# A ring of 13 one-megabyte parts for the expert weights, 96 places for the second busiest expert, and down weights read as two adjacent rows per partition

## The reference, cut to what matters

```
logits = t @ router                      # 256 x 1024 @ 1024 x 8
top_logits, top_idx = top_k(logits, 2)
gates = softmax(top_logits)
combine = sum(one_hot(top_idx, 8) * gates[..., None], axis=1)
for e in range(8):                       # D_EXPERT = 3584
    out += combine[:, e:e+1] * ((silu(t @ w_gate[e]) * (t @ w_up[e])) @ w_down[e])
```

## Time and profile before

| | us |
|---|---|
| median of 3 runs | 3119.64 (3118.27 to 3120.79) |
| the profiled execution's own time | 3116.49 |
| its span | 3114.6 |
| TensorE busy in the span | 2967.0 (95%) |
| VectorE, ScalarE busy | 1220.9 and 482.5 |
| moved by DMA | 637.05 MB, mean 205 GB/s |
| HBM read | 632.70 MB |

### The profile page before, as it was taken

One profiled execution on the slowest core, in us unless ns is written; L12 is line 12 of the kernel. 1 busy time (PEld: TensorE's weight loads), 2 busy tenths in 40 slices (PEclk: granted clock), 3 DMA queues, 4 the chain that ended last, 5 costly groups with the idle time before them and its releaser, 6 DMA issues.

```text
span 3114.6 us, 48006 instructions
## 1 busy us (share of the span) xinstructions
PE 2967.0 (95%) x20333; PEld 2077.3 (67%) x20333; DVE 1220.9 (39%) x2557; ACT 482.5 (15%) x1080; POOL 109.9 (4%) x122
## 2 busy tenths in 40 slices
PE   7999998999999999999999999998999999989987
PEld 3566666588697677696786795876667667445443
DVE  2566766457476433466465375232000100100101
ACT  2332333010010123200221200221000000000001
POOL 1111112000000000000000000000000000000000
PEclk8999999999999999999999999998999999999999
DMA  7333116465455522355310365324999899999996
GB/s 255 117 109 129 55 55 254 166 215 163 135 185 168 161 69 74 94 195 171 104 52 21 107 205 176 115 61 177 367 386 381 327 387 382 371 393 389 360 394 256
DMA packets 361238, 637.05 MB, mean 205 GB/s; under 512 B 11950, under 2 KB 190741, under 8 KB 353725
## 3 DMA queue, kind: packets, MB, share of 16 engines
q1 hardware_dynamic: 355677, 612.49, 55.6%
q0 software_dynamic: 5344, 21.46, 2.1%
HBM read 632.70 MB, written 1.20 MB: 204 GB/s over the span
## 4 chain that ended last, share of the span: by engine, by line
PE 78%; DMA 11%; DVE 4%; SPq 2%; ACT 2%; issue 2%; DVEq 1%; PEld 1%; PEldq 0%; ACTq 0%
PE PS L1087 11%; PE PS L1646 7%; PE PS L1107 7%; PE PS L4140 7%; DMA scratch<-in_moe_wu 5%; PE PS L1040 4%; DMA W<-in_moe_wu 4%; PE PS L4201 3%; PE PS L4187 2%; PE PS L4147 2%; SPq L3998 2%; PE PS L710 2%; PE PS L2222 2%; PE PS L3594 2%; PE PS L1121 2%
## 5 line engine op out<-in xcount | busy, mean ns | idle before, releaser
L1646 PE MATMUL PS<-XT,WH 128*128 128x512 f32 x512 | 241.4, 597 | 1.7 <-ACT XT L487 1.7
L4140 PEld LDWEIGHTS PS<-scratch,W 128*128 128x128 f32 x1792 | 207.5, 194 | 32.1 <-issue 32.1
L4140 PE MATMUL PS<-scratch,W 128*128 128x128 f32 x1792 | 210.1, 277 | 8.2 <-DMA W<-in_moe_wu 8.2
L4160 PE MATMUL PS<-W,scratch 128*32 128x256 f32 x2688 | 151.1, 383 | 12.9 <-DMA W<-in_moe_wu 12.9
L4160 PEld LDWEIGHTS PS<-W,scratch 128*32 128x32 f32 x2688 | 96.9, 111 | 70.5 <-issue 26.9
L1015 DVE TENSOR_TENSOR scratch<-scratch,PS 128x128 f32<-128x128 f32 x56 | 16.1, 288 | 322.2 <-ACT scratch L1005 322.2
L1087 PE MATMUL PS<-XT,W 128*128 128x128 f32 x1024 | 128.2, 280 | 12.8 <-DVEq L1260 12.8
L1040 PE MATMUL PS<-XT,W 128*128 128x256 f32 x640 | 139.6, 379 | 0.0
L1087 PE MATMUL PS<-scratch,W 128*128 128x128 f32 x1024 | 135.5, 275 | 0.0
L1646 PEld LDWEIGHTS PS<-XT,WH 128*128 128x128 f32 x512 | 89.2, 192 | 69.1 <-issue 66.6
L1040 PEld LDWEIGHTS PS<-XT,W 128*128 128x128 f32 x640 | 121.4, 190 | 18.9 <-issue 2.9
(11 more groups left out here) (620 smaller groups left out, 4805.8 us busy)
## 6 DMA issues: line engine op xcount, KB each, us to landing
W<-in_moe_wg SPq DMA_DIRECT2D x56, 1024.0 KB, 8.5
W<-in_moe_wu SPq DMA_DIRECT2D x56, 1024.0 KB, 12.9
W<-in_moe_wd SPq DMA_DIRECT2D x56, 1024.0 KB, 9.8
XT<-in_moe_wg SPq DMA_DIRECT2D x56, 1024.0 KB, 11.4
scratch<-in_moe_wu SPq DMA_DIRECT2D x56, 1024.0 KB, 14.4
OT<-in_moe_wd SPq DMA_DIRECT2D x56, 1024.0 KB, 14.0
W<-in_ada_w SPq DMA_DIRECT2D x36, 1024.0 KB, 7.0
W<-in_ffn_w_gate SPq DMA_DIRECT2D x66, 512.0 KB, 4.9
```

What stands on the lines that cost most here:

```text
L1646: mm = k.nc.tensor.matmul(k.PS[:, n % 2, :], k.gdn_w[n][:, kb, :], k.XT[:, kb, :], start=kb == 0, stop=kb == KB - 1)
L4140: mm = nc.tensor.matmul(k.PS[:, 4 + f, w * SLOTS:(w + 1) * SLOTS], slots[w].wide[:, kb, c:c + P], k.xte[:, MANY, kb, :], start=kb == 0, st ...
L4160: mm = k.nc.tensor.matmul(k.PS[j * GROUP:(j + 1) * GROUP, 4 + g // 2, g % 2 * L:g % 2 * L + L], k.xte[:, MANY, kb, g * GROUP:(g + 1) * GRO ...
```

## The change

It replaces the expert stage's loads, buffers and order of work.

- The room of the four slots becomes a ring of 13 parts of 1 MB (2048 floats in each of 128 partitions): 7 in `W`, 2 each in `XT` and `OT` and 2 in `scratch`. Each load waits only until the part that it overwrites is used (`k.used`, one count per part, in the order in which TensorE works), and TensorE waits for each part by itself (`landed`).
- A pair has 4 turns instead of 7: three of 1024 hidden columns and one of 512 (`WIDTHS`). A part of up weights holds gate and up of one block of 128 input rows, 1024 columns each (rows of 4 KB), or of two blocks, 512 columns each.
- A part of down weights in a turn of 1024 holds, in each partition, two adjacent rows of the matrix, 8 KB that lie together in HBM. It is issued as two loads of 64 partitions each. In a turn of 512 it is two loads of 128 partitions with rows of 4 KB, as before.
- All ups of both kinds come first in a turn, then all downs. Gathers, the scatters of the pair before and the turned gates stand at fixed places between MANY's up parts of the first two turns.
- All tokens are stationary in groups of 32: four groups in pair 0 (128 places), three in pairs 1 to 3 (96), two for FEWER (64). `FULL_PAIRS` is 1. PSUM banks are given anew; the down sums are added to `ye` on VectorE once per turn.
- The branch for what has no place gets a ninth round, for rank 1.

```diff
-FULL_PAIRS = 2
+FULL_PAIRS = 1
-PAIR_ROUNDS = EXPERT_PAIRS * E_TURNS
+WIDTHS = (1024, 1024, 1024, 512)
+PART = 2048
+RING = 13
+UP_FILLS = [KB * w // 1024 for w in WIDTHS]
+DOWN_FILLS = [w // 256 for w in WIDTHS]
+STEP_FILLS = [2 * (u + d) for u, d in zip(UP_FILLS, DOWN_FILLS)]
+PAIR_FILLS = sum(STEP_FILLS)
...
+def expert_ups_sync(k, sp, pair, turn, kind, e):
+    ups, _ = expert_weights(k)
+    width, first = WIDTHS[turn], sum(WIDTHS[:turn])
+    kbs = 1024 // width
+    for i in range(UP_FILLS[turn]):
+        fill = fill_at(pair, turn, "up", kind, i)
+        if fill >= RING:
+            sp.wait_ge(k.used, fill - RING + 1)
+        to = k.ring[fill % RING].rearrange("p (kb w n) -> p kb w n", kb=kbs, w=2)
+        for w in range(2):
+            src = ups[w][:, ds(e, 1), kbs * i:kbs * i + kbs, first:first + width].rearrange("p e kb n -> p (e kb) n")
+            sp.dma_start(to[:, :, w, :], src).then_inc(k.ring_in[fill % RING][0], 16)
+
+def expert_downs_sync(k, sp, pair, turn, kind, e):
+    _, downs = expert_weights(k)
+    whole = k.t["moe_wd_1_2"].rearrange("e (b p f) n -> p e b (f n)", p=P, f=2)
+    block = sum(WIDTHS[:turn]) // P
+    for i in range(DOWN_FILLS[turn]):
+        fill = fill_at(pair, turn, "down", kind, i)
+        if fill >= RING:
+            sp.wait_ge(k.used, fill - RING + 1)
+        if WIDTHS[turn] == 1024:
+            for half in range(2):
+                src = whole[:, ds(e, 1), block // 2 + i, :].rearrange("p e n -> p (e n)")
+                sp.dma_start(k.ring[fill % RING][ROWS[half], :], src[ROWS[half], :]).then_inc(k.ring_in[fill % RING][0], 16)
+            continue
+        to = k.ring[fill % RING].rearrange("p (b n) -> p b n", b=2)
+        for f in range(2):
+            b = block + 2 * i + f
+            sp.dma_start(to[:, f:f + 1, :], downs[:, ds(e, 1), b:b + 1, :].rearrange("p e b n -> p (e b) n")
+                         ).then_inc(k.ring_in[fill % RING][0], 16)
...
+def expert_up_tensor(k, pe, pair, turn, kind, i):
+    fill = fill_at(pair, turn, "up", kind, i)
+    width = WIDTHS[turn]
+    kbs, part = 1024 // width, width // 4
+    pe.wait_ge(*landed(k, fill))
+    weights = k.ring[fill % RING].rearrange("p (kb w n) -> p kb w n", kb=kbs, w=2)
+    for n in range(kbs):
+        kb = kbs * i + n
+        for g in range(groups_of(kind, pair)):
+            for j in range(4):
+                mm = k.nc.tensor.matmul(k.PS[j * GROUP:(j + 1) * GROUP, 4 * kind + g, 0:2 * part],
+                                        k.xte[:, kind, kb, g * GROUP:(g + 1) * GROUP],
+                                        weights[:, n, :, j * part:(j + 1) * part], start=kb == 0, stop=kb == KB - 1)
+    mm.then_inc(k.used, 1)
...
 def duo_step_tensor(k, pe, pair, turn):
+    for i in range(UP_FILLS[turn]):
+        expert_up_tensor(k, pe, pair, turn, MANY, i)
...
+    if n:
+        pe.wait_ge(*k.turn_dve.at("y1", n - 1))
+    for i in range(UP_FILLS[turn]):
+        expert_up_tensor(k, pe, pair, turn, FEWER, i)
+        if i == 2:
+            expert_flip_tensor(k, pe, pair, turn, MANY)
+    pe.wait_ge(*k.turn_act.at("ht0", n))
+    if n:
+        pe.wait_ge(*k.turn_dve.at("y0", n - 1))
+    for i in range(DOWN_FILLS[turn]):
+        expert_down_tensor(k, pe, pair, turn, MANY, i)
+        if i == (0 if last else 1):
+            expert_flip_tensor(k, pe, pair, turn, FEWER)
+            if last and pair + 1 < EXPERT_PAIRS:
+                duo_gather_tensor(k, pe, pair + 1, MANY)
+    pe.wait_ge(*k.turn_act.at("ht1", n))
+    for i in range(DOWN_FILLS[turn]):
+        expert_down_tensor(k, pe, pair, turn, FEWER, i)
+        if last and i == 0 and pair + 1 < EXPERT_PAIRS:
+            duo_gather_tensor(k, pe, pair + 1, FEWER)
```

More of the change, by code:

```diff
@@ L3969, with groups_of, fill_at, landed @@
 MANY, FEWER = range(2)
-def turn_slots(k, kind, n):
-    base = MOE_BASE if kind == MANY else (0, 0)
-    return k.expert_slots[2 * kind:2 * kind + 2], [n + b for b in base]
+def groups_of(kind, pair):
+    return 2 if kind else 4 if pair < FULL_PAIRS else 3
+def fill_at(pair, turn, what, kind, i):
+    at = pair * PAIR_FILLS + sum(STEP_FILLS[:turn]) + i
+    if what == "down":
+        return at + 2 * UP_FILLS[turn] + kind * DOWN_FILLS[turn]
+    return at + kind * UP_FILLS[turn]
+def landed(k, fill):
+    sem, base = k.ring_in[fill % RING]
+    return sem, base + 32 * (fill // RING + 1)
+def used(k, pair, turn, what, kind):
+    fills = UP_FILLS if what == "up" else DOWN_FILLS
+    return k.used, fill_at(pair, turn, what, kind, fills[turn] - 1) + 1
 def expert_weights(k):
@@ L3989, in moe_sync @@
                    for rank in (pair, pair + MANY_RANKS)]
-        for turn in range(E_TURNS):
+        for turn in range(len(WIDTHS)):
             for kind, e in enumerate(experts):
[L3992 to L4002, removed]
+                expert_ups_sync(k, sp, pair, turn, kind, e)
+            for kind, e in enumerate(experts):
+                expert_downs_sync(k, sp, pair, turn, kind, e)
@@ L4005, in more_sync @@
 def more_sync(k, sp):
[L4006 to L4009, removed]
+    sp.wait_ge(k.used, EXPERT_PAIRS * PAIR_FILLS)
     with sp.Fori(0, EXPERTS) as e:
         with sp.Fori(0, E_TURNS) as j:
[L4012 to L4016, removed]
@@ L4121, in scatter_tensor @@
     else:
-        pe.wait_ge(*k.ga_act.at("tr", min(e + 1, EXPERTS - 1)))
+        pe.wait_ge(*k.ga_act.at("tr", min(e + 1, NE - 1)))
         pe.wait_ge(*k.sc_dve.at("y", e))
     scatter_products(k, e % 2, tile).then_inc(*k.sc_pe.done(f"sc{tile}"))
[L4127 to L4149, removed]
@@ L4152, in tri_up_tensor @@
[L4152 to L4164, removed]
@@ L4167, in tri_flip_tensor @@
[L4167 to L4191, removed]
@@ L4194, in few_up_tensor @@
[L4194 to L4202, removed]
-                                        slots[w].wide[:, kb, s * ROUND:(s + 1) * ROUND],
-                                        start=kb == 0, stop=kb == KB - 1)
-        mm.then_inc(*slots[w].pe.both("up0", "up1"))
@@ new lines, with expert_down_tensor @@
+DOWN_PLACES = {
+    4: [(half, g, f, g, half) for f in range(2) for half in range(2) for g in range(4)],
+    3: [(0, j, f, g, half) for f in range(2) for j, (g, half) in enumerate(((0, 0), (1, 0), (2, 0), (0, 1)))]
+    + [(1, j, f, g, 1) for j, (f, g) in enumerate(((0, 1), (0, 2), (1, 1), (1, 2)))],
+    2: [(0, 2 * half + g, f, g, half) for f in range(2) for half in range(2) for g in range(2)],
+}
+def expert_down_tensor(k, pe, pair, turn, kind, i):
+    fill = fill_at(pair, turn, "down", kind, i)
+    groups, blocks = groups_of(kind, pair), WIDTHS[turn] // 512
+    last = DOWN_FILLS[turn] - 1
+    pe.wait_ge(*landed(k, fill))
+    weights = k.ring[fill % RING].rearrange("p (b n) -> p b n", b=2)
+    places = DOWN_PLACES[groups]
+    for n, (bank, j, f, g, half) in enumerate(places):
+        at = ((2 * i + f) % blocks * groups + g) * P + (2 * i + f) // blocks * GROUP
+        opens = (bank, j) not in [q[0:2] for q in places[:n]]
+        closes = (bank, j) not in [q[0:2] for q in places[n + 1:]]
+        mm = k.nc.tensor.matmul(k.PS[j * GROUP:(j + 1) * GROUP, 5 if kind else 6 + bank, :], k.ht[kind][:, at:at + GROUP],
+                                weights[:, f, half * 512:(half + 1) * 512], start=i == 0 and opens, stop=i == last and closes)
+    mm.then_inc(k.used, 1)
@@ L4577, in duo_step_vector @@
+def duo_step_vector(k, dve, pair, turn):
+    first = turn == 0 and pair
+    if first:
+        duo_scatter_vector(k, dve, pair - 1, MANY, 0)
+        duo_scatter_vector(k, dve, pair - 1, MANY, 1)
+        duo_scatter_vector(k, dve, pair - 1, FEWER, 0)
     if turn == 2 and pair + 1 < EXPERT_PAIRS:
@@ L4579, in duo_step_vector @@
             duo_choice_vector(k, dve, pair + 1, kind)
-    if turn == E_TURNS - 1:
-        for kind in range(2):
-            duo_sum_vector(k, dve, pair, kind)
+    expert_hidden_vector(k, dve, pair, turn, MANY)
+    if first:
+        duo_scatter_vector(k, dve, pair - 1, FEWER, 1)
+    expert_hidden_vector(k, dve, pair, turn, FEWER)
+    for kind in range(2):
+        expert_sum_vector(k, dve, pair, turn, kind)
 def moe_vector(k, dve):
```

336 lines of the change are left out of this document (119 added, 217 removed).

## The result

The changed kernel takes 3297.65 us, the kernel before beside it 3120.22 us (3118.27 to 3122.96): a ratio of 1.0562, interval 1.0541 to 1.0582, so 5.6% slower. It was forecast slower, by 70 us and not by 177, and the time lies above the range.

A forecast was written before the change was run, and what follows sets the result against it. Loads were taken to bind every pair: 618.4 + 401.0 = 1019.4 us from 2142.8, ending at 3162.2; plus about 4 for the last part, 18.5 after the last pair, 1.9 and 3.15 gave 3190 us, range 3034 to 3258.

The forecast's parts named there:

- the price of the half loads: 8 KB down rows, 100.7 MB: 251 GB/s, mean of three earlier windows with half loads, so 401.0 us, 166 more than at 429.
- the predicted stream of 1019.4 us: Expert-stage loads: 618.4 us for ups and other downs plus 401.0 us for 8 KB down rows, binding in every pair.
- The bounds: 8 KB down rows: 429 GB/s if half loads cost nothing (234.7 us), 214 if halves never overlap (470.4 us, kernel 3259, chance 0.15).
- Direction and mechanism: Expert stage: half loads slow the stream below 305 GB/s, TensorE waits for downs; slower, chance 0.51, 3190 us, own range 3145 to 3262.
- The break-even near 305 GB/s: 8 KB down rows: half loads at about 305 GB/s take 330 us, giving 3119, the time of now; chance 0.02.
- The 3251: 8 KB down rows by the skill's port rule, about 218 GB/s for 64 partitions: downs 462 us, kernel about 3251 us.
- Rival 1: Half loads cost nothing in the stream (853.1 us), so TensorE sets the end: 3051 us, from 3035 to 3070; chance 0.36.
- rival 2: Neither row length nor halves matter; the stage stays at 388 GB/s: 3078 us; with rates between 305 and 400, chance 0.11.
- TensorE's sum: TensorE's work in the expert stage: pairs of 244.4, 211.2, 212.8 and 205.3 us, together 873.7 us, ending alone at 3027.5.
- every cover was free: Silu, copies and adds of y in the expert stage hide behind other work, costed at 0; without cover 30 to 50 us.
- TensorE's clock: TensorE in the expert stage: granted clock at the upper level, 2.4 GHz, throughout; at the lower its work would double and bind.
- SP's queue: Load issues in the expert stage: 672, about 1.1 us a part against 2.5 us of streaming, so hidden.

The follow-up runs named there:

- the lower half alone: The changed kernel, but of each down part with 8 KB rows only the load to partitions 0 to 63 is written: 3163.44 us.
- the run with whole loads: The changed kernel, but each down part of a 1024-column turn is one load of 128 partitions instead of two of 64: 3042.45 us, ratio 0.9746.
- The kernel with the middle alone: The changed kernel, but of each down part with 8 KB rows only the load to partitions 32 to 95 is written: 3015.29 us.
- the one with middle and outer loads: The changed kernel, each down part with 8 KB rows in three loads, to partitions 32-95, 0-31 and 96-127: 3248.31 us, ratio 1.0396.

## Why the prediction was wrong

**The step that failed** is the price of the half loads, "the mean of the three windows, 251 GB/s ... 401.0 us", and that only they were priced lower. First, the value: in the middle of the first stretches it is 229, and 100.7 MB / 229 = 439.7 us, 39 more; by the mean of 239 over the whole stage it is 421 us, 20 more. The windows of the earlier trace rows fall from 262 to 238, and a mean over them took in the fall; that the whole loads in them flatter the half loads is likely, but not shown. Second, only the half loads' own bytes were priced. The 33.9 MB beside them, 83 us at my 410 GB/s, were slowed with them. In all the stretches took 572.9 us where the prediction had 401.0 + 83 = 484: 89 us more, of which 20 are the value, by the mean of 239, and 69 the neighbours. This second part is the larger one, and the prediction had it at nothing. The other 218 MB took some 12 us more than priced. That is 101 us: the predicted stream of 1019.4 us is the measured 1120.5 (2146.7 to 3271.2, less 4 at the end). A first issue 3.9 us later than in the earlier trace rows, and a median 6.0 us above the profiled execution where I had added 3.15, make it the 108 between 3190 and 3298.

**The bounds.** The lower one, 214 GB/s for the half loads and 410 for all else, gave 3259. It was no bound, since it left the neighbours at full rate: 470.4 + 83 = 553 us for the stretches that took 573. Nor was 214 the least that a half load can get: the lower half alone falls to 188. And the stated range ended at 3258, short of this bound and of the 3262 of the forecast's own range, without a reason.

**Direction and mechanism** held: stretches at full share and a low rate, TensorE waiting for downs. The direction was given a chance of 0.51, so it is no proof of much. The break-even near 305 GB/s no run tests, and it too left the neighbours out. The 3251 that I had worked out from the Trainium skill's figure of about 218 GB/s (page SBUF — State Buffer, section Door 1: The DMA port swizzle) is nearer than my 3190, in part by luck: 218 is below the 239 measured, which hides some of what the neighbours cost.

**Rival 1** (halves cost nothing) and **rival 2** (the stage stays at 388) were ruled out by the run with whole loads, which shows what rival 1 was about: 3042 against its 3051. In the earlier trace rows I misread one value: the last of the 12 slices is 256 and lies outside 327 to 394, which changes no sum.

**TensorE's sum** was 873.7 us; it is 840.7. The kernel with the middle alone shows it without a wait, busy for the whole of every pair:

```profile
2154.10:2395.60 241.50, 241.50 (x2398) 88.55 (x2394) 17.33 (x28) 15.71 (x24) 0.00 (x0) 1.00 0.94 355
2395.60:2597.90 202.30, 202.30 (x1966) 72.69 (x1962) 21.26 (x32) 13.40 (x23) 0.00 (x0) 1.00 0.96 365
2597.90:2802.70 204.80, 204.80 (x1970) 73.11 (x1966) 21.28 (x32) 13.40 (x23) 0.00 (x0) 1.00 0.96 370
2802.70:2994.80 192.10, 192.10 (x1857) 64.32 (x1853) 17.75 (x19) 12.52 (x20) 0.00 (x0) 1.00 0.87 332
```

Against 244.4, 211.2, 212.8 and 205.3. From pair 1 on each window begins two up parts late, so pair 0's holds 5 us of pair 1 and pair 3's lacks 5; put right, the sum had 8 or 9 us too much in every pair. So the kernel with whole loads ends its last pair at 3022.0, near the predicted 3027.5, for the wrong reason: the sum was 33 us too long, and 27 of the 867.9 us that its stage takes go when the loads are lighter. The same trace takes the sum apart. Parts that follow each other in pair 2, of 32, 16 and 24 records:

```profile
2649.84 3.62 PE L4251 MATMUL PS<-XT,WH 128*32 128x512 f32 x32
2653.27 1.90 PE L4251 MATMUL PS<-OT,WH 128*32 128x512 f32 x16
2654.99 2.76 PE L4205 MATMUL PS<-OT,scratch 128*32 128x512 f32 x24
2657.56 2.76 PE L4205 MATMUL PS<-scratch 128*32 128x512 f32 x24
```

By their starts they take 3.43, 1.72 and 2.57 us, where the earlier trace rows had given 3.57, 1.79 and 2.65 to 2.78. Over the four pairs that is about 25 of the 33 us; 5 are transposes (0.16 us each and not 0.19), and most of the rest is scatters. That every cover was free (silu, copies, the adds of y) is shown by the same rows: no pair has idle time.

**TensorE's clock** was taken at the upper level throughout. It was 0.93 to 0.96 in the four pairs; what that cost, with the loads binding, no run shows.

**SP's queue** was hidden, as costed: two loads of 128 partitions per part, with the same 672 issues, lose 6 us against one load at most. **The 96 places** were rightly taken as worth nothing while the loads bind.

## What to carry to other kernels

Before a load is cut, look at which partitions each piece reaches, not at how many: pieces that take every second partition cost 2 us here and pieces that take all partitions and part of the columns 6, pieces below and above partition 64 cost 255 us of 3042. A slow kind of load is priced with everything that stands in the queue beside it. And when a full resource is relieved, take the other full one's measured stage time, since the gain of 78 us was set by TensorE in pairs 0 and 1 and by the loads in pairs 2 and 3, and not by either alone.

## What the runs showed of the hardware beyond that

- Loads in one queue take on each other's pace: 4 KB packets to all partitions took 237 to 315 ns inside the half-load stretches, 164 outside, and the quick middle load ran at 231 GB/s beside the outer ones. The stretches grew from 41.0 us to 52.9 over the stage, with more of other loads in them. That the 16 DMA engines drift apart and mix more loads would fit; no run takes this apart.
- Halves in alternation gave 229 GB/s in the first stretches, 239 on average and 303 in one window, and not twice the 190 to 210 of one side. Why the rate varies so is open. Whether the order in one queue holds them back is open: halves on two queues weren't tried.
- Two kernels, the changed one and the one with middle and outer loads, each had a single execution of 11.4 and 12.8 ms. No other kernel had one, and its cause is open.
